# Attention heads taken in pairs: the fp32 products of two heads in one row, in an fp32 hybrid decoder layer on one core

## What is computed

```python
proj = x @ w_in                      # 2048 -> 512 (c_q) + 256 (c_kv) + 64 (k_idx) + 16 (w_idx)
c_q, c_kv = rms_norm(c_q), rms_norm(c_kv)
score = sum_h w_idx[h] * relu(q_idx[h] @ k_idx.T)      # 16 indexer heads, causal
sel = top_k(score, 64)                                 # keys of each query
for h in range(16):
    s = (q[h] @ k[h].T) * scale      # q[h] = c_q @ w_uq[h];  k[h] = c_kv @ w_uk[h].T
    p = softmax(s over sel)
    o[h] = p @ (c_kv @ w_uv[h])
x = LN(alpha * x + concat(o) @ w_out)
x = LN(alpha * x + (silu(x @ w_gate) * (x @ w_up)) @ w_down)
```

## Time and profile before

| | us |
|---|---|
| median of 3 runs (lowest, highest) | 956.27 (956.21, 956.43) |
| the profiled execution, its own time | 956.68 |
| its span from first to last instruction | 954.9 |
| stage of the heads on PE, first scores to last values | about 82.5 to 153.8 |

### The profile page before, as it was taken

How to read it: one execution, slowest core, us unless ns; L and a number is a source line. 1 busy time by engine, 2 the same in 40 slices (tenths; PEclk the granted TensorE clock), 3 DMA queues, 4 the chain that set the end, 5 groups by cost and what they waited for, 6 DMA issues and landing times.

```text
span 954.9 us, 12295 instructions
## 1 busy us (share of the span) xinstructions
PE 948.5 (99%) x4516; PEld 795.1 (83%) x4516; DVE 633.2 (66%) x1010; ACT 442.7 (46%) x572; POOL 40.6 (4%) x41
## 2 busy tenths in 40 slices
PE   8999999999999999999999999999999999999998
PEld 7999988888888888888888888888888888888886
DVE  5678566588777766777777766777775454554556
ACT  5686765463444444444444444444444343343450
POOL 0205530000000000000000000000000000000000
PEclk9999999999999999999999999999999999999999
DMA  9744324583365555455455555555557465464632
GB/s 337 310 174 144 123 89 176 186 351 140 118 218 205 193 185 210 176 202 194 176 178 203 206 203 179 209 183 191 182 205 290 144 230 189 161 237 153 227 126 88
DMA packets 27840, 183.57 MB, mean 192 GB/s; under 512 B 3104, under 2 KB 3232, under 8 KB 8352
## 3 DMA queue, kind: packets, MB, share of 16 engines
q1 hardware_dynamic: 27776, 183.12, 53.8%
q0 software_dynamic: 32, 0.00, 0.0%
HBM read 181.01 MB, written 2.10 MB: 192 GB/s over the span
## 4 chain that ended last, share of the span: by engine, by line
PE 99%; DMA 1%; DVE 0%; ACT 0%; SPq 0%; issue 0%
PE acc L1272 82%; PE acc L1210 5%; PE acc L1146 4%; PE acc L1409 2%; PE acc L1244 1%; PE tp L1323 1%; PE tp L1258 1%; DMA raw<-in_x_w 1%; PE tp L1336 1%; PE tp L1349 0%; PE tp L1348 0%; PE tp L1347 0%; PE tp L1365 0%; PE tp L1502 0%; PE tp L1499 0%; PE tp L1178 0%
## 5 line engine op out<-in xcount | busy, mean ns | idle before, releaser
L870 DVE TENSOR_TENSOR w_lo<-raw,w_hi 128x1024 fp32r<-128x1024 f32 (+1 forms) x283 | 335.3, 1193 | 242.5 <-ACT w_hi L618 240.7
L618 ACT ACTIVATE w_hi<-raw 128x1024 fp32r<-128x1024 f32 (+1 forms) x276 | 285.7, 1036 | 403.2 <-PE acc L1272 401.2
L1272 PE MATMUL acc<-w_hi,act_t 128*128 128x512 f32 x1344 | 413.9, 389 | 0.0
L1272 PEld LDWEIGHTS acc<-w_hi,act_t 128*128 128x128 f32 x1344 | 252.3, 188 | 52.4
L1272 PE MATMUL acc<-w_lo,act_t 128*128 128x512 f32 x672 | 261.4, 389 | 0.0
L1272 PE MATMUL acc<-w_hi,hid_t 128*128 128x512 f32 x672 | 207.2, 389 | 0.0
L1272 PEld LDWEIGHTS acc<-w_lo,act_t 128*128 128x128 f32 x672 | 126.2, 188 | 26.1
L1272 PEld LDWEIGHTS acc<-w_hi,hid_t 128*128 128x128 f32 x672 | 126.2, 188 | 26.0
L1272 PE MATMUL acc<-w_lo,hid_t 128*128 128x512 f32 x336 | 130.7, 389 | 0.0
L1017 DVE STREAM_TRANSPOSE turned<-hid 32x128 f32<-32x128 f32 x352 | 106.6, 303 | 5.6
L1272 PEld LDWEIGHTS acc<-w_lo,hid_t 128*128 128x128 f32 x336 | 63.1, 188 | 13.2
(11 more groups left out here) (180 smaller groups left out, 746.8 us busy)
## 6 DMA issues: line engine op xcount, KB each, us to landing
raw<-in_w_gu SPq DMA_DIRECT2D x88, 1024.0 KB, 4.8
raw<-in_w_down SPq DMA_DIRECT2D x32, 1024.0 KB, 4.8
raw<-in_w_out SPq DMA_DIRECT2D x16, 1024.0 KB, 4.8
raw<-in_w_down SPq DMA_DIRECT2D x16, 768.0 KB, 4.1
raw<-in_x_w SPq DMA_DIRECT2D x15, 552.0 KB, 7.2
raw<-in_w_uq SPq DMA_DIRECT2D x4, 1024.0 KB, 5.8
raw<-in_w_ukv SPq DMA_DIRECT2D x4, 1024.0 KB, 5.2
ln_rows<-in_ln_rows SPq DMA_DIRECT2D x4, 1024.0 KB, 7.5
```

The lines of the kernel that those rows point to most:

```text
L618: act.activation(w_hi[:, (2 * slot + half) % RING, 0:n], raw[:, slot, first:first + n], ACT.Copy).then_inc(hi_done, 1)
L870: dve.tensor_tensor(w_lo[:, h, 0:n], raw[:, slot, first:first + n], w_hi[:, h, 0:n], ALU.subtract).then_inc(lo_done, 1)
L1272: last = pe.matmul(acc[:, bank0 + t, :], lhs[:, k, x, t * P:(t + 1) * P], part[:, w, n * GC:(n + 1) * GC], start=(start and x == 0 and par ...
```

## The change

Two slots become one block, s = 0, 2, 4, ... 18. Each engine's steps are the same instructions in another order; none is added or removed. PE does in a row: transposes of head s-2, values of head s-3, scores of head s, transposes of head s-1, scores of head s+1, values of head s-2; then the two pieces (or the `out_k`s) of both slots. ACT: copy of probabilities s-2, `o_hi` of s-3, copy s-1, exponentials of s, `o_hi` of s-2, exponentials of s+1, then for both slots `take_piece` and `hi_static`. DVE: `o_lo` of s-3, mask and minima of s and of s+1, `o_lo` of s-2, reciprocal of s (for heads from 12 on with the normalisation), a `lo_static`, reciprocal of s+1, a `lo_static`. POOL's list is unchanged.

```diff
@@ scalar @@
-            for s in range(HEADS + 4):
-                if s >= 4:
-                    act.wait_ge(pv_full, s - 3)
...
+            for s in range(0, HEADS + 4, 2):
+                prob_turned(s - 2)
+                head_hi(s - 3)
+                prob_turned(s - 1)
+                exps(s)
+                head_hi(s - 2)
+                exps(s + 1)
+                for h in (s, s + 1):
+                    if h in PIECE_OF:
+                        take_piece(PIECE_OF[h])
+                    if h in SPLIT_OF:
+                        hi_static(SPLIT_OF[h])
@@ vector @@
-            for s in range(HEADS + 4):
...
+            def inverse(s):
+                if s < HEADS:
+                    dve.wait_ge(exp_done, 2 * s + 2)
+                    if s >= 2:
+                        dve.wait_ge(prob_done, 2 * (s - 1))
+                    dve.reciprocal(row_inv[:, (s + 1) % 2, :], row_sum[:, s % 2, :]).then_inc(inv_done, 1)
+                    if s >= POOL_NORM:
...
+            for s in range(0, HEADS + 4, 2):
+                head_lo(s - 3)
+                masked_min(s)
+                masked_min(s + 1)
+                head_lo(s - 2)
+                inverse(s)
+                if s == 0:
+                    dve.wait_ge(lo_done, 2 * R_GROUP + 8)
+                    lo_static(2 * R_GROUP + 8)
+                early_lo(s - 2)
+                inverse(s + 1)
+                if s == 0:
+                    lo_static(2 * R_GROUP + 9)
+                early_lo(s - 1)
+            early_lo(HEADS + 2)
@@ tensor @@
-            for s in range(HEADS + 3):
...
+            for s in range(0, HEADS + 4, 2):
+                turn_prob(s - 2)
+                weigh(s - 3)
+                scores(s)
+                turn_prob(s - 1)
+                scores(s + 1)
+                weigh(s - 2)
+                for h in (s, s + 1):
+                    if h in PIECE_OF:
+                        piece(PIECE_OF[h])
+                    for k in out_parts.get(h, ()):
+                        out_k((k,), 0)
```

More of the change, by code:

```diff
@@ L589, in _, with prob_turned, head_hi, exps @@
             hi_static(2 * R_GROUP + 9)
-            for s in range(HEADS + 4):
-                if s >= 4:
-                    act.wait_ge(pv_full, s - 3)
[L595 to L598, removed]
+            def prob_turned(u):
+                if 0 <= u < HEADS:
+                    act.wait_ge(pt_full, u + 1)
+                    act.activation(prob_t[:, u % 2, :], tp[:, 2, 0:KEYS], ACT.Copy).then_inc(pt_done, 1)
+            def head_hi(u):
+                if 0 <= u < HEADS:
+                    act.wait_ge(pv_full, u + 1)
+                    act.activation(o_t[:, u, 0, :], tp[:, 3, 0:S], ACT.Copy).then_inc(o_hi, 1)
+            def exps(s):
                 if s < HEADS:
@@ L828, in _, with head_lo, masked_min @@
             dve.wait_ge(bias_done, 1)
-            for s in range(HEADS + 4):
[L831 to L834, removed]
+            def head_lo(u):
+                if 0 <= u < HEADS:
+                    dve.wait_ge(o_hi, u + 1)
+                    dve.tensor_tensor(o_t[:, u, 1, :], tp[:, 3, 0:S], o_t[:, u, 0, :], ALU.subtract).then_inc(o_lo, 1)
+            def masked_min(s):
                 if s < HEADS:
@@ L839, in _ @@
                                              op1=ALU.add).then_inc(neg_done, 1)
[L840 to L844, removed]
                     dve.wait_ge(neg_done, s + 1)
@@ L848, in _, with early_lo @@
                            .then_inc(min_done, 1)
[L849 to L852, removed]
+            def inverse(s):
[5 more added lines that the diff above has]
+                    if s >= POOL_NORM:
+                        dve.wait_ge(inv_done, s + 1)
+                        dve.wait_ge(prob_done, 2 * s)
+                        for t, cols in blocks:
+                            dve.tensor_scalar(prob[:, s % 3, cols], prob[:, s % 3, cols],
+                                              row_inv[:, (s + 1) % 2, t:t + 1], None, ALU.mult).then_inc(prob_done, 1)
+            def early_lo(s):
+                if s in SPLIT_OF:
+                    lo_static(SPLIT_OF[s])
+            for s in range(0, HEADS + 4, 2):
[4 more added lines that the diff above has]
+                inverse(s)
                 if s == 0:
@@ L1315, in _, with scores @@
                          18: (10, 11)}
-            for s in range(HEADS + 3):
+            def scores(s):
                 if s < HEADS:
@@ L1325, in _, with turn_prob @@
                     last.then_inc(qk_full, 1)
[L1326 to L1331, removed]
+            def turn_prob(u):
+                if 0 <= u < HEADS:
                     pe.wait_ge(prob_done, 2 * u + 2)
@@ L1338, in _, with weigh @@
                     last.then_inc(pt_full, 1)
-                if s >= 3:
-                    u = s - 3
+            def weigh(u):
+                if 0 <= u < HEADS:
                     g, h = divmod(u, GH)
```

## The result

The changed kernel takes **966.48 us** (median of 4 executions, 966.35 to 968.09) against 956.35 for the kernel before in the same job (4, 956.21 to 956.51): ratio 1.0108, interval 1.0096 to 1.0120. It is slower, by 10.1 us. The forecast was 963.9 with a range to 965.8, so the sign is right, the size some 2.6 us too small, and the time outside the range.

A forecast was written before the change was run, and what follows sets the result against it. PE, busy for 99% of the span, was taken to bound the kernel. Terms 2.3 + 2.4 + 2.2 + 0.85 - 0.15 = 7.6 us on a median of 956.27 gave 963.9 us, range 961.8 to 965.8.

The forecast's parts named there:

- What bounds the kernel, and that lead is what the change spends: Whole kernel: PE's list is the time, PE 99% busy; operands are ready ahead, and the change spends that lead.
- Changes from fp32 to fp32r, 0.15 gained: On PE: ten type changes instead of 20, five of those removed lying in each part, 0.03 each, 0.15 us gained.
- Rival 4: No slower: the 0.58 us row is true cost on PE, so ten changes give 1.9 us back; chance 0.04.
- Block 2, 2.3 by ACT's list: Block 2: transposes of head 1 wait for ACT's copy of head 0, wanted at 90.38, ready at 92.70; 2.3 us late.
- POOL's delay lies inside it: Block 2: POOL's delay of head 0 adds nothing to the 2.3 us, as ACT's list does not depend on it.
- Blocks 4, 6, 8, 10, 0.6 each: Transposes of head s-1 wait for ACT's copy of head s-2's probabilities; 0.6 late, four times, 2.4 us.
- Block 16, 0.85: Block 16: head 15's transposes 0.2 late behind ACT, head 14's values wait for DVE's `o_lo`; together 0.85 us.
- Block 12, POOL held twice, 2.2: Block 12: transposes of head 10 wait for POOL, both of whose instructions start inside a `w_lo`; 2.2 us late.
- so all of it stays: The sum: PE is the only bound behind the stage to the end, so the whole 7.6 us remains.
- PE's busy time should stay within 0.3 us: Sign for the changed kernel's profile; a change of PE's busy time over 1 us would make the prediction wrong.
- Rival 2: Block 12: DVE is held by POOL too, PE waits until 9.28, 0.4 more, 964.3 us; chance 0.15.
- Rival 1: Block 12: POOL is not held by DVE, or only once; costs 0.55 to 1.45, 962.3 to 963.2 us; chance 0.2.

The follow-up runs named there:

- the last kernel: Changed kernel with heads 10 and 11 on DVE, last `w_hi` later, ACT's blocks 0 and 2 handwritten, two early reciprocals, `out_k` 8 moved in block 16: 957.21 us.
- ACT's order changed: Changed kernel, but ACT copies the probabilities of head s-2 before the last `w_hi` of the block: 965.51, 965.52, 965.52 and 963.74 us, ratio 1.0090.
- long wait: Kernel before, with PE made to wait after head 15's values for a POOL memset of 2048 columns: 958.74 to 960.47 us, ratio 1.0032.
- the filled wait: Changed kernel, with ten unused fp32r matmuls on PE ahead of the transposes of head 10: 964.89 us, ratio 1.0089.
- head 10 ahead: Changed kernel, but in block 10 DVE takes both reciprocals first and starts its `w_lo`s only after POOL normalised head 10: 964.37 us, ratio 1.0084.
- the first repair: Changed kernel with heads 10 and 11 normalised on DVE and ACT's last `w_hi` of a block behind the next block's exponentials: 959.68 us, ratio 1.0036.

## Why the prediction was right or wrong

- *What bounds the kernel, and that lead is what the change spends*: right. Each wait named came at its place, and the time comes back with the waits.
- *Changes from fp32 to fp32r, 0.15 gained*: right. Where two or four `out_k`s stand in a row each takes 0.01 less. Rival 4, the 0.58 row as true cost, is refuted by the last kernel, which has nine fewer changes, hardly a wait, and no gain. The row starts under the product before it: a long row in a pipelined engine is no cost until the chain shows it.
- *Block 2, 2.3 by ACT's list*: 2.2 measured, and ACT's list ends the last wait, as I said. But it is one of two limits a quarter of a microsecond apart: with ACT's order mended POOL, held once in each of its first two instructions by the block's `w_lo`s (1.51 and 1.63), is late by 2.0 all the same. "POOL's delay lies inside it" was true of the sum and would have misled a repair; only the last kernel, which mends both, brought the term down, to 0.4.
- *Blocks 4, 6, 8, 10, 0.6 each*: 0.61 each, right. *Block 16, 0.85*: 0.8, right.
- *Block 12, POOL held twice, 2.2*: the mechanism right, the size 0.2 short. I let POOL in between the two `w_lo`s, 0.13 before the first one's end, and held its second instruction again. In the trace the first instruction is held through both (2.61 in blocks 4 to 12, five of five) and the second is free (0.91): 3.5 for the pair instead of my 3.13. The handover from POOL to PE is some 0.1 shorter than the 0.32 that I took from DVE. What I had described, one `w_lo` at a time, is what block 2 shows, and no other block.
- **The step that failed** is the sum itself, in the sentence "so all of it stays", which priced a wait at its own length and nothing more. Behind block 12's 2.4 us PE ran 3.4 us at the lower clock and lost 1.65. No term and no rival spoke of the clock; "PE's busy time should stay within 0.3 us" took it for granted. The runs show it: with PE kept busy through the same wait the time is 1.6 lower, and with the wait gone 4.2. With that term and the 0.2 of POOL, 963.9 becomes 965.8; the rest of 0.7 is half in what I have not placed and half in that the jobs' medians and the profiled executions differ by a few tenths.
- *Rival 2, DVE held too*: not seen where it mattered. In block 12 POOL did not get in between the two `w_lo`s, and the second of them took 1.21. In block 2, where it did, the second `w_lo` took 1.32, 0.1 more and not the 0.4 to 0.5 of the rival. The Trainium skill (SBUF — State Buffer, section "Who interferes with whom") has a DVE instruction with two SBUF inputs and a GpSimd one that reads SBUF contend, and the order of issue decide who blocks. That POOL blocks, the trace confirms with 2.61 against 0.60; that an instruction at the head of one queue is let in between two back-to-back ones of the other engine, on which my 2.2 rested, the rows show in one block of six (block 2). Nor do engines wait for each other on semaphores alone, as the description of the chip above has it: no semaphore stands between a `w_lo` and POOL's instruction.
- *Rival 1, POOL not held*: refuted by the same row.

## What to carry to other kernels

In a kernel bound by one engine, write down for every order change how late each producer becomes, list by list; this gave six of seven terms here to 0.1 us. Then ask of the longest wait what the clock of TensorE does behind it, and let the range reach to that: a wait of 2.4 us cost 4.1. And when two engines contend, as POOL and DVE here, an instruction of the one that yields may have to outlast the whole back-to-back run of the other, so bound the term by the run and not by one instruction.

## What was unexpected of the hardware

- **The clock behind a wait.** The three profiled falls of the granted clock (changed kernel, ACT's order changed, long wait) go to the lower level (1.2 GHz) 0.5 to 0.8 us after the end of an idle stretch of PE, and the price is 1.4 to 1.8 us. With a wait of 2.3 us by the waits view, or of 2.5 (ACT's order changed), seven of eight executions had a lower mean clock; with 1.9, three of seven; with one of 1.1, none of ten. Block 2's waits of 1.4 and 0.5 close together may do it as well: four kernels that keep them (DVE normalising head 10, the filled wait, head 10 ahead, the first repair) have each one execution of four or five with a mean clock of 0.998, 1.3 to 1.9 us longer, and the last kernel, without them, has none of eleven. The kernel before, which has no wait of PE in this stage, has one of 32. The executions of the four kernels with the lower clock have no trace, so where their clock fell is not shown, and that block 2 is the place is a guess. The changed kernel's own 968.09 has a mean clock of 0.996 against 0.998 in its three others, which fits one more fall.
- **POOL outlasting a run of DVE.** An instruction of 0.60 us takes 2.61 when it starts inside the first of two `w_lo`s with no gap between them; I had expected 1.55, and a hold of the second instruction. With head 10 ahead one of 0.92 takes 2.71. With 0.18 us between the `w_lo`s it is let in (1.50). Block 2, let in without such a gap (1.51), is the exception, and its cause is open.
- **The other way round it hardly costs.** In block 2 a `w_lo` beside POOL's instructions took 1.32, and with head 10 ahead one that starts 0.05 us into POOL's 0.60 took 1.39, instead of 1.21; DVE was never seen held for a whole instruction of POOL.
